# The gates of an RG-LRU layer as 64-row products in the two halves of the TensorE array

## What is computed

```python
def rg_lru(x, w_a, b_a, w_x, b_x, lam):
    xh = xf.reshape(bsz, s, LRU_HEADS, LRU_HEAD_DIM)
    r = sigmoid(einsum('bshi,hij->bshj', xh, w_a).reshape(bsz, s, D_LRU) + b_a)
    i = sigmoid(einsum('bshi,hij->bshj', xh, w_x).reshape(bsz, s, D_LRU) + b_x)
    log_a = -LRU_C * r * softplus(-lam)
    a = exp(log_a)
    mult = sqrt(-expm1(2.0 * log_a))
    h = associative_scan(a, mult * (i * xf))
```

## Time and profile before

| | us |
|---|---|
| median of 3 runs | 2148.7 |
| lowest and highest of them | 2148.31, 2149.93 |
| span of the profiled execution, first to last instruction | 2147.1 |
| PE busy in it | 2116.0 |
| DVE busy | 1466.8 |
| ACT busy | 867.6 |

### The profile page before, as it was taken

The page is one execution under the profiler, slowest core; times in us unless marked ns, Lnnn a source line. Parts: engine busy times, 40 slices in busy tenths (PEclk is TensorE's granted clock), DMA queues, the critical chain, the costliest instruction groups (busy, mean ns, idle before and its releaser), DMA issues.

```text
span 2147.1 us, 24298 instructions
## 1 busy us (share of the span) xinstructions
PE 2116.0 (99%) x9296; PEld 1746.0 (81%) x9296; DVE 1466.8 (68%) x1679; ACT 867.6 (40%) x1128; POOL 365.7 (17%) x684
## 2 busy tenths in 40 slices
PE   8999999999999999999999999999999999999996
PEld 6888888888888888888888888888888888888884
DVE  7885497685858677688786743874655656574866
ACT  5764364352525344355445622522313131323342
POOL 0101002111112211221100111122222222222210
PEclk9999999999999999999999999999999999999998
DMA  5436546566657556576533364466666666666643
GB/s 223 162 142 261 179 167 242 203 250 218 243 193 268 220 212 235 218 288 245 191 124 135 98 215 131 145 191 193 194 194 192 194 195 195 190 194 196 211 152 108
DMA packets 134994, 419.08 MB, mean 195 GB/s; under 512 B 15456, under 2 KB 15584, under 8 KB 134880
## 3 DMA queue, kind: packets, MB, share of 16 engines
q0 software_dynamic: 91776, 318.81, 42.8%
q1 hardware_dynamic: 40800, 90.33, 12.8%
q10 hardware_dynamic: 2304, 8.39, 1.0%
HBM read 244.46 MB, written 173.02 MB: 194 GB/s over the span
## 4 chain that ended last, share of the span: by engine, by line
PE 97%; DVE 1%; DMA 1%; ACT 0%; SPq 0%; issue 0%; DVEq 0%; ACTq 0%
PE slot L660 47%; PE slot L807 38%; PE slot L887 11%; DMA XN<-xT 1%; PE slot L725 1%; DVE H L2159 0%; PE slot L738 0%; PE slot L749 0%; DVE wpair L1499 0%; DMA split_panels<-wpair 0%; DVE wsum L1493 0%; SPq L558 0%; DVE WV L2150 0%; DVE XQ L2154 0%; DVE WV L2152 0%
## 5 line engine op out<-in xcount | busy, mean ns | idle before, releaser
L807 PE MATMUL slot<-ops,wpair 128*128 128x512 f32 x3696 | 841.9, 390 | 0.7 <-ACT WG L1225 0.4
L807 PEld LDWEIGHTS slot<-ops,wpair 128*128 128x128 f32 x3696 | 693.6, 188 | 147.0 <-ACT WG L1225 3.0
L660 PE MATMUL slot<-Uhi,wpair 128*128 128x512 f32 x1248 | 339.7, 391 | 10.5 <-DVE wpair L1499 8.6
L620 POOL DMA_DIRECT2D split_panels<-wpair x274 | 146.1, 534 | 840.0 <-DVE wpair L1499 815.4
L660 PEld LDWEIGHTS slot<-Uhi,wpair 128*128 128x128 f32 x1248 | 234.7, 188 | 60.9 <-issue 9.5
L645 POOL DMA_DIRECT2D wpair<-split_panels x262 | 141.2, 539 | 753.0 <-PE slot L660 346.6
L660 PE MATMUL slot<-f_split,wpair 128*128 128x512 f32 x1152 | 262.1, 389 | 0.0
L660 PEld LDWEIGHTS slot<-f_split,wpair 128*128 128x128 f32 x1152 | 216.4, 188 | 44.7
L887 PE MATMUL slot<-f_quarter,wpair 128*128 128x512 f32 x1008 | 229.5, 389 | 0.0
L887 PEld LDWEIGHTS slot<-f_quarter,wpair 128*128 128x128 f32 x1008 | 189.3, 188 | 39.2
L965 ACT ACTIVATE wpair<-raw 128x512 fp32r<-128x512 f32 x186 | 113.4, 624 | 253.4 <-PE slot L660 168.2
(11 more groups left out here) (197 smaller groups left out, 2298.4 us busy)
## 6 DMA issues: line engine op xcount, KB each, us to landing
split_panels<-wpair POOLq DMA_DIRECT2D x274, 512.0 KB, 4.6
wpair<-split_panels POOLq DMA_DIRECT2D x262, 512.0 KB, 3.6
raw<-panels SPq DMA_DIRECT2D x208, 256.0 KB, 4.2
wpair<-down_sums POOLq DMA_DIRECT2D x48, 256.0 KB, 2.9
wlo_sum<-down_sums POOLq DMA_DIRECT2D x48, 256.0 KB, 3.0
down_sums<-raw POOLq DMA_DIRECT2D x36, 256.0 KB, 3.2
H<-xT SPq DMA_DIRECT2D x8, 1024.0 KB, 10.4
pp_kept<-XQ ACTq DMA_DIRECT2D x16, 512.0 KB, 3.7
```

What stands on the lines that cost most here:

```text
L620: pool.dma_start(split_d[n], wpair[n % RING][:].bitcast(F32)).then_inc(split_kept[n % RING], 16)
L660: mm = pe.matmul(ps[:, h * BANK:(h + 1) * BANK], stat_[:, w], mov(part, h), start=first and i == 0, stop=last and i == 2)
L807: mm = pe.matmul(ps, stat_[:, w], (lo if part else hi)[:, k, :], start=first and k == 0 and i == 0, stop=k == KP - 1 and i == 2, skip_grou ...
```

## The change

The two gates of a group are no longer two jobs of 128-row products, but one function, `gates`, of 64-row products. The panel holds one block for both gates: on rows 0 to 63 the first head's a weights (columns 0 to 63) and x weights (columns 64 to 127), on rows 64 to 127 the second head's x weights and a weights, in the opposite columns. Slot a receives the products of rows 0 to 63, slot x those of rows 64 to 127, in turn. So slot a holds gate a of head 0 above gate x of head 0, and slot x holds gate x of head 1 above gate a of head 1. There are still 12 matmuls of 512 columns in a group, each with 64 rows of weights and data, alternating between the two halves of the array. ACT applies four sigmoids of 64 partitions where it had two of 128, in part from one half of the partitions to the other. PE waits for both slots before the first product, and ACT for both gates before the first sigmoid.

```diff
+            def gates(b, m):
+                keys, n = ((b, "a", m), (b, "x", m)), PANEL[b, "small", m]
+                pe.wait_ge(*split(n))
+                pe.wait_ge(gates_in, b * GROUPS + m + 1)
+                for key in keys:
+                    pe.wait_ge(*free(key))
+                for at_pass, (stat_, part) in enumerate(passes(n)):
+                    for h in range(HALVES):
+                        for e, key in enumerate(keys):
+                            rows = slice(e * HEAD, (e + 1) * HEAD)
+                            mm = pe.matmul(psum(key)[:, half_of(h)], stat_[rows, 0:P],
+                                           (Ylo if part else Yhi)[rows, 2 * m + 1, half_of(h)],
+                                           start=at_pass == 0, stop=at_pass == 2)
+                            if at_pass == 2 and h == HALVES - 1:
+                                mm.then_inc(pe_step, 1)
...
-                    small(b, "a", 0, 2 * m + 1, m, gates_in)
-                    small(b, "x", 1, 2 * m + 1, m, gates_in)
+                    gates(b, m)
...
-                    act.wait_ge(pe_step, STEP[a])
-                    nc.scalar.activation(R, psum(a)[:], ACT.Sigmoid, bias=col("b_a", m)).then_inc(slot_free[SLOT[a]], 1)
                     act.wait_ge(pe_step, STEP[x])
-                    nc.scalar.activation(I, psum(x)[:], ACT.Sigmoid, bias=col("b_x", m)).then_inc(slot_free[SLOT[x]], 1)
+                    left, right = slice(0, HEAD), slice(HEAD, P)
+                    nc.scalar.activation(R[left], psum(a)[left, :], ACT.Sigmoid, bias=col("b_a", m)[left])
+                    nc.scalar.activation(R[right], psum(x)[right, :], ACT.Sigmoid, bias=col("b_a", m)[right])
+                    nc.scalar.activation(I[left], psum(a)[right, :], ACT.Sigmoid, bias=col("b_x", m)[left]
+                                         ).then_inc(slot_free[SLOT[a]], 1)
+                    nc.scalar.activation(I[right], psum(x)[left, :], ACT.Sigmoid, bias=col("b_x", m)[right]
+                                         ).then_inc(slot_free[SLOT[x]], 1)
 
                     act.wait_ge(*out_of(a))
+                    act.wait_ge(*out_of(x))
...
-                out[r, rows, 1, rows] = w_x[m * (P // d) + e]
+                out[r, rows, 0, other] = w_x[m * (P // d) + e]
```

More of the change, by code:

```diff
@@ L23 @@
 LRU_C = 8.0
+HEAD = 64
 EPS = 1e-6
@@ L2197, in pack_panels @@
                 rows = slice(e * d, (e + 1) * d)
+                other = slice(P - (e + 1) * d, P - e * d)
                 out[r, rows, 0, rows] = w_a[m * (P // d) + e]
-                out[r, rows, 1, rows] = w_x[m * (P // d) + e]
+                out[r, rows, 0, other] = w_x[m * (P // d) + e]
             out[r, :, 2, :] = w_pool[POOL_ORDER[m]]
```

## The result

| | before | after |
|---|---|---|
| median us (runs) | 2149.07 (4) | 2162.25 (4) |
| ratio, 95% interval | | 1.006, 1.0046 to 1.0074 |
| profiled span us | 2147.1 | 2158.2 |

Slower, as forecast, but by 11 to 13 us where 5.8 stood: outside the range of 2151.0 to 2158.0. The profiled execution is the shortest of the four after the change (2160.26 us), so the trace accounts for 11.1 us of the loss. Why the first set lies 1.8 us above the second is open. In the kernel after the lines of before stand some 20 lower: L1522 is the L1499 of before, L1533 the L1510, L1639 the L1616, L1663 the L1640.

A forecast was written before the change was run, and what follows sets the result against it. Two nearly even lines were taken to bound the kernel: PE's matmuls and a chain ACT, DVE, PE. Block 0's +4.25 and block 1's +1.5 gave 5.8 us, so 2154.5 us, range 2151.0 to 2158.0.

The forecast's parts named there:

- two lines nearly even: Mixer: PE's matmuls and a chain ACT, DVE, PE are nearly even; the change shortens the first and lengthens the second.
- from above, 1.00. I take 1.00.: ACT's gates: a 64-partition sigmoid costs at most 1.00 us, as a full one; lower bound 0.52.
- the 2.15 of the forecast: ACT's line, each group: two more sigmoids add 2.00 us, the tanh's wait for the last 0.15.
- The forecast's one-element-per-lane argument: ACT's sigmoids: an activation does one element per cycle and lane, so half the lanes save nothing.
- the rival of half-cost sigmoids: ACT's half-height sigmoids cost 0.52 each, so the kernel gets faster, 2145.3 us; 0.09, shared with overlooked slack on ACT's line.
- The saving of 1.36: PE's gates: two 64-row products overlap fully, saving 1.36 us per group, 10.9 over 8 groups.
- at most about 0.16 each: PE's gates: each of two switches of the array's division per group costs at most about 0.16 us.
- nothing later gives it back: After block 0, which ends at +4.25 us: PE stands only 0 to 0.6 us at a time until block 1.
- the forecast's 0.25 for the late hi part: Block 1, L1640 of group 3: 0.25 us later because ACT's own two more sigmoids delay its hi part.
- The clock rival: PE's clock falls in the three longest new waits, 1.7 us lost each: +5, 2159.5 us; chance 0.09.
- the main forecast: Whole kernel: full or nearly full overlap and 1.00 us per sigmoid give 2154.5 us, give or take 1.3; chance 0.66.
- No overlap: PE's gates: 64-row products overlap little or not at all, 2155.3 to 2155.8 us; chance 0.16.

The follow-up runs named there:

- the first set: The first four runs of the changed kernel, median 2162.25 us against 2149.07 before; the second set is five more runs, 2161.24 against 2149.84.
- e3: Changed kernel with idle products filling three of PE's waits, which end no later for it; 2158.91 us, +9.3 against the kernel before.
- e2: Kernel before with its 128-row products, but each gate's sigmoid in two pieces of 64 rows, after both products; 2161.47 us, +11.8.
- e4: Kernel before with two extra full-height sigmoids per group, so four of 128 rows in a row, after both products; 2156.86 us, +7.2.
- e5: The changed kernel again, nothing else changed; 2161.24 us, +11.4 against the kernel before.
- e8: Changed kernel with each group's 64-row products not alternating: all six of one array half, then all six of the other; 2161.95 us, +12.1.
- e11: Kernel before with four half-height sigmoids and nine idle products in the wait before group 0's pool product of both blocks; 2160.49 us, +11.1.
- e6: Changed kernel with the four sigmoids reordered: both writing partitions 0 to 63, then both writing 64 to 127; 2162.06 us, +12.2.
- e7: Changed kernel with two ACT copies that PE waits for moved between the sigmoids and the tanh; 2150.21 us against 2149.84 before.
- e12: The kernel of e9 once more, for the interval; 2148.16 us against 2149.41 for the kernel before, ratio 0.9994.
- e9: e7 plus group 3's pooled copy before its tanh and DVE reading the next P projection before its wait; 2147.98 us against 2149.43 before.

## Why the prediction was right in kind and wrong in size

The mechanism stood: two lines nearly even, PE's saving lost at the first pool product, ACT's line longer, no slack at the ends of the blocks. Place by place, PE's start after minus before:

| place | forecast | measured (after) | wait forecast, measured |
|---|---|---|---|
| block 0, pool product of group 0 | +2.15 | +2.60 | 3.5, 3.30 |
| gates of group 3 | +3.04 | +4.22 | 3.6, 3.21 |
| G3 | +3.5 | +4.82 | 1.8, 0.64 |
| pool product of group 3 | +4.25 | +6.01 | |
| block 1, pool product of group 0 | +6.2 | +8.84 | 3.3, 3.04 |
| gates of group 3 | +5.4 | +10.32 | 1.9, 1.71 |
| G3 | +5.0 | +9.90 | |
| pool product of group 3 | +5.8 | +11.10 | |

(The forecasts of block 1 are its terms on top of 4.25. The wait before G3 of block 0 is short because the gates ahead of it ran at half clock; at full clock, in e3, it was 1.65.)

```profile
166.88 0.62 PE L661 MATMUL slot<-Yhi,wpair 128*128 128x512 f32 x2
```
```profile
1231.47 0.73 PE L772 MATMUL slot<-Yhi,wpair 64*128 64x512 f32 x4 [1.71 <-issue]
...
1233.77 0.73 PE L661 MATMUL slot<-Uhi,wpair 128*128 128x512 f32 x2 [0.64 <-DVE WV L1533]
```
```profile
1245.85 0.70 PE L661 MATMUL slot<-Yhi,wpair 128*128 128x512 f32 x2 [0.91 <-issue]
```

*The step that failed first*: "from above, 1.00. I take 1.00." The upper bound was taken from the spacing of full sigmoids, which holds an overlap of 0.10 us; without that overlap each costs its length, and the term is 2.57 (changed kernel, 2.58 in e2), where full-height sigmoids have the 2.15 of the forecast (e4). The row for it was there: the duration, 1.11, beside the spacing, 1.00. An upper bound on a cost has to drop the overlap too. The forecast's one-element-per-lane argument was right, and with it the rival of half-cost sigmoids fell: the other side of the sign was excluded for the right reason.

*The saving of 1.36* was 0.90. The bound on a switch, "at most about 0.16 each", came from a row on another thing; a switch cost 0.23. It is a small error, since PE's time in the gates counts at one place per block.

*Together*: put 2.57 and 0.90 into the forecast's own steps. In block 0 three groups' sigmoids stand ahead of L1616 of group 2 and of L1640 of group 3, so they come 3 x 0.42 later: +5.9 and +5.5 (measured 5.84 and 5.37 after, 6.14 and 5.67 in e3). In block 1: +2.57 at L1640 of group 0, 2.57 - 0.26 - 0.90 = +1.4 at L3, 1.4 + 2.57 = +4.0 at L1616 of group 2, and 4.0 - 0.56 + 0.25 - 0.88 = +2.8 at the pool product of group 3. e3's shifts there, less the 6.66 with which it enters the block, are +2.58, +1.52, +4.10 and +3.26; in the last step the forecast's 0.25 for the late hi part measured 0.56 (from +10.23 to +10.79 in e3). Between the blocks 0.7 to 1.2 us more came in, where the forecast had "nothing later gives it back" and no more loss; all of it was not traced. The sum is 5.5 + 2.8 + 0.7 to 1.2, so 9.0 to 9.5, and e3 measured +9.3 in the median. That alone comes to about the upper end of the range, 2158.0, which is +9.3; the clock carried the time past it.

*The clock rival* was given 0.09 and happened. It was right in mechanism: two of its three longest waits had a fall behind them, of 6.8 and 3.4 us. Its price of 5 was too high, 1.6 to 2.1 by e3 and e5, as the fall in block 0 leaves next to nothing at the end and only the one in block 1 counts. That rival and the main forecast were treated as exclusive, with its 9 in 100; it was an addition to every case that has these waits, and the range had to reach over it. New waits of 3.3 to 3.6 us, between 1.5 where the clock stayed and 6.4 where it fell, spoke for a chance near one in two, not one in eleven.

*No overlap*: the overlap exists. That it would hardly matter is borne out by e8 and e11. *Half-cost sigmoids*: 0.2 + 0.2 - 1.36 is -1.0, not "near -1.2", so that rival's time was 2145.5; nothing hangs on it.

## What to carry to other kernels

Before a saving on the busiest engine is counted, look at who releases its next instruction: where an operand arrives 0.10 us before it is used, the saving ends in a wait and instructions added to that operand's line are paid for, here with a loss of 11 us where the matmuls alone promised a gain of 7. What the added instructions cost depends on what stands behind them in their queue: the same four sigmoids cost 11 us less once the copies that TensorE waits for stood ahead of the tanh. And for a kernel whose tensor engine never waits, each new wait of the lengths seen here, 2.0 to 3.3 us, should carry a possible fall of the clock in the range of the forecast, on top of every case that has the wait.

## What the runs showed of the hardware

- Activations of 64 partitions by 1024 took 1.10 us as those of 128 did, but did not overlap: 1.10 to 1.14 apart against 1.00, in any order of halves (changed kernel, e2, e6 against e4). Half the lanes cost more than all, 0.43 us for four.
- Two 64-row products ran at once, 12 in 1.59 us against 2.72. Each switch of the division cost 0.23 us, with 0.35 us of idle weight loading. Without alternation they still overlapped in part, 2.16 us (e8), and the second half's first product started before the first half's fourth.
- The length of a wait did not tell whether the clock fell. It fell behind waits of 3.21 and 3.04 (changed kernel; in e5 and e6 the same two waits, 3.21 to 3.23 and 3.05 to 3.06), 3.01 (e7), 2.48 and 2.11 (both e8), 2.40 (e2) and 2.00 (e12). It stayed up behind 3.30 (changed kernel), 3.34 (e5), 3.31 (e6) and 2.78 (e8), all at the first pool product, where it fell behind e2's 2.40, and behind 2.15 (e2, block 1), 2.06 (e9) and 2.00 (e4). e9 and e12 are the same kernel and the wait is the same one. The Trainium skill ("TensorE: Matmul & The Clock Gate", HAM oscillation) has a pause throw the clock back; the traces agree that it happens, and show that among pauses of 2.0 to 3.3 us the longer one may be spared. Products whose result nobody reads kept it up in all of the stage (e3).
